# A decoder trunk on eight cores: the order of the first loads and the dummies of the opening, changed

## What is computed

```python
xn = rmsnorm(h, norm_g)
q, k, v, ga, u, gb, alow, mg = split(xn @ w_in)            # 512 512 1024 1024 512 512 16 2048 columns
la = log_sigmoid(alow @ w_alpha + b_alpha) / 16            # the forget gate, per token and key channel
o, S_new = gla_scan(q * 128**-0.5, k, v, la, S0, chunk)    # gated linear attention, 4 heads, state 128 x 256
ya = (rmsnorm_per_head(o) * gla_gain * silu(ga)) @ w_a
yb = (pool_mix(u, pool_w) * pool_scale * silu(gb)) @ w_b   # trailing means over 2, 4, 8, 16 tokens
h = h + (sigmoid(mg_a) * ya + sigmoid(mg_b) * yb) @ w_out
```

## Time and profile before

| | us |
|---|---|
| median of 3 runs | 1123.73 (1122.69 to 1123.86) |
| the profiled execution, its own time | 1122.94 |
| its span, first to last instruction of the slowest core | 1121.4 |
| spans of the eight cores | 1118.8 to 1121.4 |
| mean granted TensorE clock of the cores | 0.993 to 0.995 of 2.4 GHz |
| TensorE busy, slowest core | 1092.8 (97%) |
| VectorE, GpSimd, ScalarE busy | 673.9, 601.6, 515.0 |
| DMA, mean | 157 GB/s of bytes written |

### The profile page before, as it was taken

One profiled execution on the slowest core, in us unless ns is written; L12 is line 12 of the kernel. 1 busy time (PEld: TensorE's weight loads), 2 busy tenths in 40 slices (PEclk: granted clock), 3 DMA queues, 4 the chain that ended last, 5 costly groups with the idle time before them and its releaser, 6 DMA issues.

```text
span 1121.4 us, 27773 instructions; the slowest of 8 cores (1118.8 to 1121.4 us)
## 1 busy us (share of the span) xinstructions
PE 1092.8 (97%) x9958; PEld 856.6 (76%) x9958; DVE 673.9 (60%) x1087; ACT 515.0 (46%) x1052; POOL 601.6 (54%) x925
## 2 busy tenths in 40 slices
PE   7999999999999999999989999999999999999996
PEld 3687777786887777778757877787788867787785
DVE  5368767655845765565554776656666376656554
ACT  2646565665432434234237465655544323433333
POOL 5178788876853433343343787787776323333332
PEclk8999999999999999999999999999999999999998
DMA  9964666674596989898687234444545966845521
GB/s 196 198 132 124 140 120 134 150 156 91 102 178 153 276 264 291 222 270 229 163 142 189 53 86 92 75 88 101 110 74 135 195 210 202 270 157 188 203 68 58
DMA packets 123210, 176.20 MB, mean 157 GB/s; under 512 B 82384, under 2 KB 89040, under 8 KB 118976
## 3 DMA queue, kind: packets, MB, share of 16 engines
q1 hardware_dynamic: 107808, 138.38, 42.3%
q0 software_dynamic: 15264, 36.05, 22.0%
HBM read 138.55 MB, written 53.01 MB: 171 GB/s over the span
## 4 chain that ended last, share of the span: by engine, by line
PE 90%; DMA 3%; issue 2%; POOL 2%; DVE 1%; ACT 1%; POOLq 0%; DVEq 0%; ACTq 0%
PE psum L562 90%; DMA arena<-w 2%; ACT arena L589 1%; POOL arena L604 1%; DVE arena L616 1%; DVE arena L604 0%; POOL arena L611 0%; DMA arena<-hin 0%; PE psum L568 0%; POOL arena L623 0%; POOL arena L636 0%; DVE arena L611 0%; POOLq L246 0%; DVEq L269 0%; DVE arena L623 0%
## 5 line engine op out<-in xcount | busy, mean ns | idle before, releaser
L562 PE MATMUL psum<-arena 128*128 128x256 bf16 (+6 forms) x9854 | 1088.7, 279 | 22.4 <-DVE arena L604 4.9
L562 PEld LDWEIGHTS psum<-arena 128*128 128x128 bf16 (+2 forms) x9854 | 850.4, 98 | 256.0 <-issue 19.6
L604 POOL TENSOR_TENSOR arena<-arena 128x256 bf16<-128x256 f32 (+12 forms) x345 | 340.4, 991 | 299.7 <-DVE arena L616 233.2
L616 DVE SCALAR_TENSOR_TENSOR arena<-arena,psum 128x256 f32<-128x256 f32 (+7 forms) x472 | 265.6, 600 | 186.8 <-PE psum L562 142.7
L589 ACT ACTIVATE arena<-psum,arena 128x256 f32<-128x256 f32 (+3 forms) x432 | 173.3, 456 | 306.0 <-PE psum L562 253.0
L589 ACT ACTIVATE arena<-psum 128x256 bf16<-128x256 f32 (+7 forms) x258 | 159.0, 630 | 183.2 <-PE psum L562 162.5
L611 POOL TENSOR_SCALAR arena<-arena 128x256 f32<-128x256 f32 (+7 forms) x378 | 169.5, 457 | 103.6 <-ACT arena L589 57.6
L589 ACT ACTIVATE arena<-arena 128x1024 bf16<-128x1024 f32 (+4 forms) x144 | 141.5, 996 | 94.4 <-DVE arena L616 50.7
L616 DVE SCALAR_TENSOR_TENSOR arena<-psum,arena 128x512 f32<-128x512 f32 (+6 forms) x195 | 125.2, 656 | 62.0 <-PE psum L562 50.9
L616 DVE SCALAR_TENSOR_TENSOR arena<-arena 128x256 bf16<-128x256 f32 (+4 forms) x124 | 112.8, 919 | 63.7 <-POOL arena L604 59.2
L636 POOL DMA_DIRECT2D arena<-w x106 | 62.3, 590 | 49.4 <-PE psum L562 32.1
(11 more groups left out here) (10 smaller groups left out, 21.3 us busy)
## 6 DMA issues: line engine op xcount, KB each, us to landing
arena<-hin SPq DMA_DIRECT2D x32, 512.0 KB, 6.9
arena<-sgla SPq DMA_DIRECT2D x16, 1024.0 KB, 8.5
nsg_s<-arena SPq DMA_DIRECT2D x16, 1024.0 KB, 6.8
arena<-w POOLq DMA_DIRECT2D x30, 512.0 KB, 14.9
arena<-w POOLq DMA_DIRECT2D x48, 224.0 KB, 5.0
arena<-XN SPq DMA_DIRECT2D x20, 512.0 KB, 5.9
H<-arena SPq DMA_DIRECT2D x16, 512.0 KB, 4.8
arena<-H SPq DMA_DIRECT2D x16, 512.0 KB, 5.0
```

The source lines that it names most:

```text
L562: return S.add("pe", lambda e: e.matmul(out, lhsT=lhsT, rhs=rhs, start=start, stop=stop, skip_group_check=sgc), r=[lhsT, rhs] + list(also_ ...
L604: return S.add(eng, lambda e: e.tensor_tensor(out=out, in0=in0, in1=in1, op=op), r=[in0, in1], w=[out], after=after, cost=c)
L616: return S.add("dve", lambda e: e.scalar_tensor_tensor(out=out, in0=in0, scalar=scalar, in1=in1, op0=op0, op1=op1), r=r, w=[out], cost=eco ...
```

## The change

1. The issues of V's parts 1 and 2 are recorded ahead of all other loads, on GpSimd's queue and without a condition. The forget-gate columns, now first of the rest, still wait for x0 (`ADV = 1`), all 14 others for the second load into `hx`.
2. On SyncE's queue the forget gate's table is loaded last instead of fifth.
3. The planner takes the landing times of the first eight SyncE loads and the first two GpSimd loads from constants (`LANDS`, us) instead of its model, and goes on from there.
4. `warm` runs once, for tile 0: the same 60 cold matmuls, now with costs of their own, then 60 "fillers" of 128x512 into a bank that is held. The 26 dummies of tiles 1 to 3 are gone. Fillers are outside the list of ready operations: whenever the operation chosen for TensorE would start at least 0.6 of a filler's cost after TensorE is free, a filler goes first. This ends when the 60 are used or when the first operation that depends on one (the bank's next user) is chosen; fillers left over are dropped. The held bank is released in recording after step D/1 (`HOLD`), and until then its partner bank isn't given out as a lone one.

```diff
--- before.py
+++ after.py
@@ -21,6 +21,10 @@
 NS = NSS * TS
 NM = NS + NMETA
 NPAIR = 8
+LANDS = dict(sp=(5.2, 5.4, 7.2, 9.5, 12.5, 15.8, 17.8, 19.0),
+             pool=(12.0, 17))
+ADV = 1
+N_FILL, HOLD = 60, "D/1"
 NTOK = SEQ + NM
 EPS = 1e-6
 IN_COLS = 6160
@@ -56,6 +60,7 @@
         self.last_w = {}
         self.readers = {}
         self.cache = {}
+        self.fillers = []
 
     def grains(self, x):
         if isinstance(x, (str, tuple)):
@@ -120,7 +125,7 @@
             self.readers[g] = []
         deps.pop(i, None)
         self.ops.append(dict(eng=eng, fn=fn, deps=deps, dma=dma, token=None, cost=float(cost), lat=float(lat),
-                             attach=attach, fine=fine))
+                             attach=attach, fine=fine, land=None))
         return i
 
     @staticmethod
@@ -134,10 +139,16 @@
         n = len(ops)
         succ = [[] for _ in range(n)]
         npred = [0] * n
+        spare = list(self.fillers)
+        idle, ends = set(spare), set()
+        todo = n - len(spare)
         for i, op in enumerate(ops):
             for d, kind in op["deps"].items():
-                succ[d].append((i, self.in_order(ops[d], op, kind)))
-                npred[i] += 1
+                if d in idle:
+                    ends.add(i)
+                elif i not in idle:
+                    succ[d].append((i, self.in_order(ops[d], op, kind)))
+                    npred[i] += 1
         ready_t = [0.0] * n
         done_t = [0.0] * n
         engs = list(self.ENGS)
@@ -147,11 +158,11 @@
         dma_free = {e: 0.0 for e in engs}
         other = {"sp": "pool", "pool": "sp"}
         for i in range(n):
-            if npred[i] == 0:
+            if npred[i] == 0 and i not in idle:
                 heapq.heappush(pend[ops[i]["eng"]], (0.0, i))
         order = []
         start_t = {}
-        while len(order) < n:
+        while todo:
             best = None
             for e in engs:
                 T = free_t[e]
@@ -166,6 +177,17 @@
                 if best is None or (st_, idx) < (best[0], best[1]):
                     best = (st_, idx, e)
             st_, idx, e = best
+            if idx in ends:
+                spare = []
+            if e == "pe" and spare and order and idx > spare[-1]:
+                late = st_ - 0.6 * ops[spare[0]]["cost"]
+                if free_t[e] < late:
+                    k = spare.pop(0)
+                    free_t[e] += ops[k]["cost"]
+                    done_t[k] = free_t[e]
+                    order.append(k)
+                    continue
+            todo -= 1
             if avail[e] and avail[e][0] == idx:
                 heapq.heappop(avail[e])
             else:
@@ -180,6 +202,9 @@
                 dma_free[e] = begin + op["cost"] + min(both, 20000.0 if op["fine"] else r * op["cost"])
                 dma_free[other[e]] += min(op["cost"], both / r)
                 done_t[idx] = dma_free[e] + 2000.0
+                if op["land"] is not None:
+                    done_t[idx] = max(op["land"], free_t[e])
+                    dma_free[e] = done_t[idx] - 2000.0
             else:
                 free_t[e] = st_ + op["cost"]
                 done_t[idx] = st_ + op["cost"] + op["lat"]
@@ -196,11 +221,14 @@
         new_ops = []
         for old in order:
             op = ops[old]
-            op["deps"] = {remap[d]: k for d, k in op["deps"].items()}
+            op["deps"] = {remap[d]: k for d, k in op["deps"].items() if d in remap}
             new_ops.append(op)
         self.ops = new_ops
 
     def finalize(self):
+        for e, t in LANDS.items():
+            for op, x in zip([op for op in self.ops if op["dma"] and op["eng"] == e], t):
+                op["land"] = 1e3 * x
         self.list_schedule()
         ops = self.ops
         for op in ops:
@@ -352,6 +380,7 @@
         self.freed = {b: b - 8 for b in range(8)}
         self.clock = 0
         self.rank = []
+        self.held = ()
 
     def pick(self, c, key):
 
@@ -366,7 +395,7 @@
         return (s, s + 1)
 
     def one(self):
-        lone = [b for b in self.freed if (b ^ 1) not in self.freed]
+        lone = [b for b in self.freed if (b ^ 1) not in self.freed and (b ^ 1) not in self.held]
         c = lone or list(self.freed)
         assert c, "no bank"
         b = self.pick(c, lambda b: (self.freed[b], b))
@@ -672,18 +701,21 @@
             r0, n = rows(t)
             return d_[r0:r0 + n, :]
 
+        W1V = [(0, O_V)] + [(O_V + 2048 * i, O_V + 2048 * (i + 1)) for i in range(8)]
         cft = f32(base, NCF)
         ones = kTs[0][:, 0:512]
         memset("dve", ones, 1.0)
         act(ss[2][:, 0:1], ones[:, 0:1], AF.Square)
+        for a, b in W1V[1:3]:
+            dma(V1[:, a:b], w1[0][:, a:b], eng="pool", rate=310.0)
         x0_ = dma(hb[0], rows_of(hin, 0))
         dma(cols, cols_d[:, :])
         dma(cft, cf_d[:, :])
         dma(hb[1], rows_of(hin, 1))
-        dma(Tst[:, 0:512], walpha_d[0])
         for t in range(2):
             x3_ = dma(hx[t], rows_of(hin, 2 + t))
         dma(hm[0:NM, :], rows_of(hin, 16))
+        dma(Tst[:, 0:512], walpha_d[0])
         cp("dve", ident_b, cft[:, CF_ID:CF_ID + 128])
         cp("dve", caus_b, cft[:, CF_CA:CF_CA + 128])
         cp("dve", maskm_b, cft[:, CF_MM:CF_MM + 128])
@@ -701,7 +733,6 @@
         memset("dve", V(rmm_b, 4, NM)[:, :, 0:NS].rearrange("p h (s t) -> p h s t", t=TS)[:, :, :, 0:1], 0.0)
         memset("dve", V(rmm_b, 4, NM)[:, :, NS:NS + 1], 0.0)
 
-        W1V = [(0, O_V)] + [(O_V + 2048 * i, O_V + 2048 * (i + 1)) for i in range(8)]
         W1R = [(2048 * i, 2048 * (i + 1)) for i in range(7)] + [(14336, N_R1)]
         W2V = [(CB // 4 * i, CB // 4 * (i + 1)) for i in range(4 * N_EARLY_C)]
         W2R = [(CB // 2 * i, CB // 2 * (i + 1)) for i in range(2 * (8 - N_EARLY_C))]
@@ -763,29 +794,34 @@
             tt("dve", dst, V(bt, 8, n), g_, ALU.mult)
             banks.free(b_)
 
-        def warm(n, cold=False):
-
-            if cold:
-                bs = [banks.pair() for _ in range(4)]
-                bk = [bank(x)[:, 512 * h:512 * h + 512] for x in bs for h in range(2)]
-                for i in range(24):
-                    r = slice(32 * (i % 4), 32 * (i % 4) + 32)
-                    mm(bk[i % 4][:, 0:256], ones[r, 0:128], ones[r, 0:256], True, True, share=4.0)
-                for i in range(16):
-                    r = slice(32 * (i % 4), 32 * (i % 4) + 32)
-                    mm(bk[4 + i % 4], ones[r, 0:128], ones[r, :], True, True, share=4.0)
-                for i in range(16):
-                    r = slice(32 * (i % 4), 32 * (i % 4) + 32)
-                    mm(bk[i // 4][r, 0:256], ones[:, 0:32], ones[:, 0:256], True, True, share=4.0)
-                for x in bs:
-                    banks.free(x)
-                n = 4
-            b_ = banks.one()
-            for i in range(n):
-                k = mm(bank(b_), ones[:, 0:128], ones, True, True)
-                if cold:
+        held = []
+
+        def warm():
+
+            bs = [banks.pair() for _ in range(4)]
+            bk = [bank(x)[:, 512 * h:512 * h + 512] for x in bs for h in range(2)]
+            for i in range(24):
+                r = slice(32 * (i % 4), 32 * (i % 4) + 32)
+                k = mm(bk[i % 4][:, 0:256], ones[r, 0:128], ones[r, 0:256], True, True)
+                S.ops[k]["cost"] = 52.0 + 1250.0 * (i == 0)
+            for i in range(16):
+                r = slice(32 * (i % 4), 32 * (i % 4) + 32)
+                k = mm(bk[4 + i % 4], ones[r, 0:128], ones[r, :], True, True)
+                S.ops[k]["cost"] = 114.0
+            for i in range(16):
+                r = slice(32 * (i % 4), 32 * (i % 4) + 32)
+                k = mm(bk[i // 4][r, 0:256], ones[:, 0:32], ones[:, 0:256], True, True)
+                S.ops[k]["cost"] = 53.0
+            for x in bs:
+                banks.free(x)
+            held.append(banks.one())
+            banks.held = held[0]
+            for i in range(4 + N_FILL):
+                k = mm(bank(held[0]), ones[:, 0:128], ones, True, True)
+                if i < 4:
                     S.ops[k]["cost"] *= 2.0
-            banks.free(b_)
+                else:
+                    S.fillers.append(k)
 
         def load_x(p, after=()):
             for t in tiles_of(p):
@@ -797,8 +833,8 @@
                 for i, t in enumerate(tiles_of(p)):
                     r0, n = rows(t)
                     h = hm[0:n, :] if t == 16 else (hx if t in (2, 3) else hb)[t % 2]
-                    if t < 4:
-                        warm((20, 9, 9, 8)[t], t == 0)
+                    if t == 0:
+                        warm()
                     norm_t(0, h, n, t, xn_of(p)[:, :, i * 128:i * 128 + n], t < 4 or t == 16)
             elif p < NPAIR:
                 dma(xnT[p % 2], XN[1][p], r=[("XN", 1, p)])
@@ -1204,7 +1240,7 @@
                     tt("dve", wal[r:r + 32, :], walf[r:r + 32, :], wal[r:r + 32, :], ALU.subtract)
                 if l == 0:
```

(7 more changed lines are left out.)

## The result

The changed kernel takes 1129.5 us (median) where the kernel before takes 1123.8 on the same chip: 1.0045 of its time, 95% interval 1.0035 to 1.0055, or 5 to 6 us slower. The forecast was 1121.0 with a range up to 1124.8; it was wrong in sign. On a second chip, beside the experiment that decided the matter, the ratio was 1.0050 (1.0037 to 1.0062).

What follows compares the result with a forecast made beforehand. TensorE bounds the kernel, and the weight stream limits the opening's gain: 1.4 us slack + 1.3 us advance = 2.7 us, so 1123.7 - 2.7 = 1121.0 us, range 1117.6 to 1124.8.

Steps and rivals of the forecast that it cites:

- What bounds the kernel: Whole kernel: TensorE-bound, 98% busy outside the opening; the weight stream limits what fixing the opening returns.
- the slack of 1.4: U's part 2: lands at 64.86 us, first used at 66.24, so TensorE can gain 1.4 us before waiting.
- the 8.9 us: TensorE before 28 us: loss from waits and half clock, 4.3 + 0.5 + 1.4 + 2.7; the most the opening could return.
- The stream's advance: Weight stream: V's parts sent early move it ahead by 0.7 to 2 us, taken as 1.3.
- equal turns at about 17: Second hx load: with queues alternating equally, it lands at 17.2 us, so V's third part lands at 24.0.
- busy without a break: Opening's DMA engines: basis of the rival that the stream doesn't move, gain 1.4 us, 1122.3; chance 0.22.
- a gap in the stream: Weights between V's parts 2 and 3: late hx load leaves engines dry, 1126.2 us; chance 0.14.
- x0's cover: Tile 0's start: x0 lands up to 2.7 us later, hidden by 1.4 us before its transposes.
- The other sign: Weight stream: the prediction is wrong if V's third part lands after 25 us.
- Fillers at 0: TensorE's opening: up to 34 more dummies, at most 7.5 us, lie in idle time and cost 0.
- The reorder at ±1 us: TensorE after 76 us: the new instruction order may move the 19.4 us idle by 1 us either way.
- the mixture: DMA engines: weights and tokens moving together save 0.7 us in 10 against each alone.

Runs made afterwards that it cites:

- run 5: Kernel before with 19 dummy matmuls put in front of V0a/0's first matmul after its order was made, nothing else moved: ratio 1.0007.
- run 2: Changed kernel with the loads of before and LANDS set to the landings measured there; planner and fillers alone: ratio 1.0081.
- run 7: Changed kernel with one V part issued early instead of two: ratio 1.0021.
- run 9: Changed kernel with V's two early parts as four pieces of 1024 columns, twice the packets for the same bytes: ratio 1.0014.
- 13: Kernel before, once its order is made, with the issue of V's part 3 also waiting for V's part 2 to land: ratio 1.0040.
- 18: Kernel before with only the added wait of V's part 3 for V's part 2, repeated on the same chip as the changed kernel: ratio 1.0048.
- run 4: Changed kernel without its 60 fillers (N_FILL = 0): ratio 1.0034.
- 6: Changed kernel with LANDS set to the landings of its own trace: ratio 1.0068.
- 11: Kernel before with the hole filled by 19 dummies and the loads X/2 and GF moved to behind GA0/0: ratio 1.0010.
- 12: Kernel before with the loads X/2 and GF moved to behind GA0/0, no dummies added: ratio 1.0018.
- 16: Kernel before with the hole filled by 19 dummies and both pair 2's tokens and the forget gate's table moved to behind Q/0: ratio 1.0048.
- run 1: Kernel before with the changed load order alone, its own planner model and dummies: ratio 1.0106.
- run 3: Changed kernel with all 15 later weight parts issued behind x0, none waiting for the second hx load (ADV = 99): ratio 1.0077, 1135.7 us.
- 14: Changed kernel with the weight parts from V's third on waiting for the first hx load instead of the second: ratio 1.0029.
- 17: Changed kernel, unchanged, timed again on another chip beside the gap alone: ratio 1.0050.

## Why the prediction was wrong

**What bounds the kernel** held. The opening is ended by the weight stream: with the hole filled TensorE came 2 us further by 28 us and no further by 76 (run 5), and run 2 gained 1 to 1.5 us of work by 76 us, about the slack of 1.4. That the 8.9 us are not what the opening returns was right. The slack itself was read on core 5 alone: cores 0 and 1 of the same trace wait 0.5 us for U's part 1 already, and have none.

**The stream's advance, taken as 1.3 us, is the step that failed**, by sign: core by core, U's part 2 went back by 3.6 to 8.7 us. It was checked by "V's third part is issued once the second hx load is in, with equal turns at about 17". Three things in that sum were off. First, it let the shared stretch move 0.222 MB/us, the mean of a stretch in which the queues moved equal bytes; from 5 to 13 us after, they moved 1.34 MB in 8 us, 0.17 MB/us, with as many packets from each (212 to 213), and SyncE's were the short ones. Second, what moves before SyncE's second hx load is added to its time in full: 1.11 MB of weights at 0.172 MB/us are 6.5 us, and 14.4 + 6.5 = 20.9, against 21.3 to 22.0 measured (20.7 to 22.2 in runs 7 and 9, with the same bytes); all numbers of this sum were in the earlier trace rows. Third, GpSimd didn't issue at the landing (21.9) but at 23.4, as the small operations of a tile stood in its queue and waited for ScalarE; on the other cores the issue came 0.5 to 1.1 us behind the landing. The engines were "busy without a break" before; the two queues' later work could be kept behind each other only if the weights' queue always held some, and the wait for the hx load left it with one packet in 6 us.

**The rival "a gap in the stream"** is what happened, at its own figure for the load, 21.7 against 21.9 in the trace; price 1126.2 forecast, 1129.5 measured. It was given 0.14, on the sum that put the load at 17.2. Runs 13 and 18 show that a wait of this size suffices: it alone costs 1.0040 and 1.0048, the changed kernel 1.0050 beside it. The price was too low by 3 us: on the slowest core V's part 3 came 5.9 us late, not 3.9 (issued 1.5 us behind the load instead of 0.3, and 7.3 us on its way instead of 6.7), and U's part 2, behind it, 8.5 us. That the rest was lost to tokens that now fell on the same stretch (the DMA share there is 1.03, it was 0.94) is likely, not shown.

**x0's cover.** The prediction followed x0 and left the constants out. x0 didn't land later (4.7 to 6.0 us); the constants behind it did, at 10.8 to 13.2 instead of 6.3 to 8.2, VectorE couldn't scale tile 0 before it had converted them, and tile 0's transposes started at 12.4 to 14.7, on four of the eight cores after 13, which the prediction named as a sign of its failure. The other sign, V's part 3 after 25 us, came true on all eight (27.0 to 30.7). The equal turns that it cited from the Trainium skill (DMA: Bandwidth & Descriptors, queues, rings and completion order) are what the trace shows, and the rows from 6 to 11 us that were held against them showed one queue alone: its rival had sent nothing yet. The Trainium skill states there that the turn is a whole packet of several descriptors, which the prediction left out; the trace, whose packets of the weights hold about one row each (0.80 MB in 212), shows near equal numbers of them from both queues, and run 9 nearly (300 to 271); how many go in one turn no run here shows.

**Fillers at 0** was right (run 4). **The reorder at ±1 us** was nearly right for this change, 1.2 us more idle behind 76 us, and that by luck: runs 2, 6, 11, 12 and 16 show orders that cost 3 to 10 us from the same operations.

**What stays open.** The loads alone cost 1.0106 (run 1), the gap alone 1.0040 to 1.0048; the rest is likely the late tokens in an order that doesn't know of them, and was not tried by itself. How the changed kernel's own loss divides between gap and tokens is open too: its slower cores wait for weights between 34 and 54 us, its quicker ones hardly, and in run 3 late tokens and tables, without the gap, cost 1.0077. The changed kernel has the late tokens too and is no slower than the gap alone; that its new order and full clock (0.94 and 1.00, against 0.86 and 0.94) pay for them fits the numbers and is argued, not shown. Ratios below 1.003 on the slower chips (runs 7, 9, 14) can't be told from the scale of those chips: the changed kernel was never timed on one, and the chip of runs 17 and 18 was a quick one (1124.1), so the rival that the change costs less where the kernel before is slow stays untested.

## What to carry to other kernels

In this kernel, with the DMA engines shared, the second hx load landed when all the bytes that moved before it, in either queue, had taken their time at the rates of their kinds, those issued after it on the other queue among them (run 7). Add them in full and don't hope for the mixture. If the issue of a stream waits for a load, the stream's start moves with that load, and the question to ask of a load moved forward is which wait stands behind what it pushes back, in every engine's queue: here GpSimd's issues behind a token load, and VectorE's scaling behind the constants. Filling a bound engine's early hole was worth no more than the slack of the next transfer (here nothing, run 5), and the test is cheap: fill the hole with dummies and look whether the waits come back.

## What was not expected of the hardware

The two queues took turns by packet: 212 to 213 packets in 8 us at 0.80 to 0.54 MB, and with weight rows half as long 300 to 271 packets at 0.55 to 0.74 MB. A load of 0.23 MB in short rows (1816 bytes) landed with a weight part of 512 KB (11.4 and 11.3 us). V's first part took 9.7 us from issue to landing when it came first, and 12.0 when SyncE's loads were ahead of it, where its queue moved nothing from 6 to 11 us. The kernel before, unchanged, took between 1123.8 and 1128.0 us on different chips, and its U's part 2 landed up to 3 us later on a slower one.
